# Feed-forward as 2x2 block products, seven in place of eight

## The reference

```python
D_FF = ((8 * D_MODEL // 3 + 255) // 256) * 256          # 2816

def swiglu_ffn(x, g, w_gu, w_down):
    h = rmsnorm(x, g) @ w_gu
    a, b = jnp.split(h, 2, axis=-1)
    return (jax.nn.silu(a) * b) @ w_down

# in each of the two layers, after the mixer:
x = x + swiglu_ffn(x, ffn_norm[layer], w_gate_up[layer], w_down[layer])
```

## Time and profile before

| | us |
|---|---|
| median of 3 runs (1864.62 to 1868.22) | 1866.26 |
| span of the profiled execution | 1864.6 |
| TensorE busy | 1815.1 |
| VectorE busy | 913.6 |
| ScalarE busy | 694.5 |
| GpSimd busy | 582.0 |

### The profile page before, as it was taken

The page is one execution under the profiler, slowest core; times in us unless marked ns, Lnnn a source line. Parts: engine busy times, 40 slices in busy tenths (PEclk is TensorE's granted clock), DMA queues, the critical chain, the costliest instruction groups (busy, mean ns, idle before and its releaser), DMA issues. The chain is left out here.

```text
span 1864.6 us, 41136 instructions
## 1 busy us (share of the span) xinstructions
PE 1815.1 (97%) x17185; PEld 1692.6 (91%) x17185; DVE 913.6 (49%) x1392; ACT 694.5 (37%) x1097; POOL 582.0 (31%) x298
## 2 busy tenths in 40 slices
PE   8999998999999999999998999999989999999998
PEld 7999997999999999999997677777779999999998
DVE  4757766345555521145653466655543555554000
ACT  5365455431221222245632555555544212222111
POOL 3333221243333343333531011221113333333332
PEclk9999999999999999999999999999999999999999
DMA  5333341222322232242356999999963222223222
GB/s 126 89 97 82 83 111 55 79 80 80 90 81 80 83 93 83 76 142 72 114 178 211 396 386 386 381 360 363 361 217 91 80 80 85 85 80 97 79 78 82
DMA packets 289101, 273.75 MB, mean 147 GB/s; under 512 B 19602, under 2 KB 250099, under 8 KB 288404
## 3 DMA queue, kind: packets, MB, share of 16 engines
q1 hardware_dynamic: 286980, 268.62, 44.1%
q10 hardware_dynamic: 1792, 1.44, 0.3%
q0 software_dynamic: 144, 1.05, 0.2%
HBM read 254.64 MB, written 16.43 MB: 145 GB/s over the span
## 5 line engine op out<-in xcount | busy, mean ns | idle before, releaser
L2020 POOL TENSOR_TENSOR a_wl<-a_wraw,a_wh 128x1024 fp32r<-128x1024 f32 (+2 forms) x91 | 233.5, 2566 | 401.1 <-ACT a_wh L1944 401.0
L2020 POOL TENSOR_TENSOR b_wl<-b_wraw,b_wh 128x1024 fp32r<-128x1024 f32 (+1 forms) x66 | 172.7, 2616 | 298.3 <-ACT b_wh L1944 298.3
L1901 PE MATMUL ps<-xh,a_wh 128*128 128x288 f32 x1104 | 238.4, 298 | 0.0
L1901 PE MATMUL ps<-xh,a_wl 128*128 128x288 f32 x1104 | 236.9, 296 | 0.0
L1901 PE MATMUL ps<-xl,a_wh 128*128 128x288 f32 x1104 | 236.8, 296 | 0.0
L1944 ACT ACTIVATE a_wh<-a_wraw 128x1024 fp32r<-128x1024 f32 (+2 forms) x91 | 100.6, 1106 | 335.5 <-PE ps L1901 315.4
L1944 ACT ACTIVATE b_wh<-b_wraw 128x1024 fp32r<-128x1024 f32 (+1 forms) x66 | 75.0, 1136 | 318.5 <-PE ps L1901 318.5
L2037 DVE TENSOR_TENSOR xT<-xT,ps 128x576 f32<-128x576 f32 x32 | 24.1, 754 | 320.8 <-PE ps L1901 320.8
L1901 PEld LDWEIGHTS ps<-xh,a_wh 128*128 128x128 f32 x1104 | 177.0, 187 | 1.1 <-issue 0.2
L1901 PEld LDWEIGHTS ps<-xh,a_wl 128*128 128x128 f32 x1104 | 177.2, 187 | 0.6
L1901 PEld LDWEIGHTS ps<-xl,a_wh 128*128 128x128 f32 x1104 | 177.2, 187 | 0.6
(11 more groups left out here) (352 smaller groups left out, 3880.6 us busy)
## 6 DMA issues: line engine op xcount, KB each, us to landing
a_wraw<-in_w_gate_up SPq DMA_DIRECT2D x44, 512.0 KB, 3.9
b_wraw<-in_w_gate_up SPq DMA_DIRECT2D x44, 512.0 KB, 3.8
xT<-in_cache_k SPq DMA_DIRECT2D x40, 512.0 KB, 6.4
xT<-in_cache_v SPq DMA_DIRECT2D x40, 512.0 KB, 6.9
a_wraw<-in_a_w_in SPq DMA_DIRECT2D x32, 512.0 KB, 4.2
f_h_plain<-in_cache_k SPq DMA_DIRECT2D x30, 512.0 KB, 6.1
xl_plain<-in_cache_v SPq DMA_DIRECT2D x30, 512.0 KB, 6.8
f_h_plain<-in_cache_v SPq DMA_DIRECT2D x30, 512.0 KB, 6.6
```

The source lines that it names most:

```text
L1901: mm = pe.matmul(ps[0:width(n), bank(n) + a, 0:HALF], wt[:, base(n) + t, 0:width(n)], ap[:, first + t, a * HALF:(a + 1) * HALF], start=kin ...
L2020: pool.tensor_tensor(part(wl, n), part(wraw, n), part(wh, n).bitcast(F32), ALU.subtract).then_inc(e["low"], 1)
```

## The change

The feed-forward's products become products of 2x2 blocks by Winograd's form of Strassen's method. A unit is now a pair: the gate and up tile of one hidden tile, or two neighbouring output tiles of the down product. Its weight is a 2x2 matrix of blocks (two column tiles; input tiles in pairs, even and odd), the activation is a 2x2 matrix too (input tiles even and odd; the two halves of the tokens), and the output's four blocks (two tiles, two halves) come from seven products instead of eight. Each product is still three matmuls of parts for each pair of input tiles: 12 matmuls for gate and up (four pairs), 9 or 6 for a down unit (three or two pairs).

Weights: seven blocks are loaded, of which four are targets of sums: S1 and S3 get A22 and a neighbour added by one transfer, S2 gets S1, S4 gets S2 (`add_operands`, transfers that GpSimd's queue issues and that add to what lies there). ScalarE rounds each operand three products ahead (`round_part`), into five slots; VectorE makes its low part two products ahead (`low_part`). GpSimd computes nothing in the feed-forward. Activations: each tile gives blocks and, for an odd one, combinations with the even one (`cross`, VectorE, one operation for an even and three for an odd tile), rounded by ScalarE (`round_combinations`) and made low by VectorE (`low_combinations`). Outputs: products share three banks a unit; of a gate-and-up unit ScalarE copies out three intermediate sums (`snapshot`) and VectorE makes the rest (`evict`), the gate in two banks of PSUM; of a down unit VectorE adds or subtracts all seven into `xT`.

The hidden width is cut in four chunks (4, 6, 6 and 6 tiles); the down product of a chunk (four units) stands behind the first gate-and-up unit of the next. The loads of unit m wait for the low parts of unit m - 2; the first unit's for the low part of output unit 7.

```diff
+A22, A11, S1, S3, A12, S2, S4 = range(7)
+
+
+def fast_products():
+
+    return ((A11, 0, 0), (S1, 1, 2), (S2, 4, 0), (A12, 2, 1), (S3, 5, 0), (S4, 3, 2), (A22, 6, 0))
...
+    chunks = [(0, 4), (4, 10), (10, 16), (16, KF)]
+    C = len(chunks)
+    ROWS = KD // 2
+    UNITS = [("o", f) for f in range(KD)]
+    for c, (first, end) in enumerate(chunks):
+        UNITS += [("g", i) for i in range(first + (1 if c else 0), end)]
+        if c < C - 1:
+            UNITS += [("g", end)]
+        UNITS += [("d", c, j) for j in range(ROWS)]
...
+    BANKS = ((0, 1, 2), (3, 6, 7))
+    SLOTS, AHEAD = 5, 3
...
+                def fetch(n):
+                    m, pairs = n - KD, pairs_of(n)
+                    if m == 0:
+                        sp.wait_ge(e["low"], KD)
+                    elif m == 1:
+                        sp.wait_ge(e["used"], KD)
+                    else:
+                        wait_low(sp, S * (m - 1))
...
+                    for dst, a, x in ((A11, 0, 0), (A22, 1, 1), (S1, 1, 0), (S3, 1, 0)):
+                        sp.dma_start(operand(m, dst), block(a, x)).then_inc(fetched[m % 2], 16)
+                    for dst, a, x in ((S2, 0, 0), (A12, 0, 1), (S4, 0, 1)):
+                        sp.dma_start(operand(m, dst), block(a, x)).then_inc(later[m % 2], 16)
...
+                    read = {2: 0, 4: 2, 5: 1, 6: 4}
+                    if pos in read:
+                        at = m, read[pos]
+                        if at in snap:
+                            pe.wait_ge(e["snapped"], snap[at] + 1)
+                        else:
+                            pe.wait_ge(e["taken"], take[at] + 1)
...
+                def product(n, pos):
+                    m, pairs = n - KD, pairs_of(n)
+                    which, b, _ = PRODUCTS[pos]
+                    s = S * m + pos
+                    banks_ready(n, pos)
+                    if pos in POOLED:
+                        pe.wait_ge(e["poollow"], m * len(POOLED) + POOLED.index(pos) + 1)
+                    else:
+                        wait_low(pe, s + 1)
+                    high, low = (slots[i][s % SLOTS] for i in range(2))
+                    for t, q in enumerate(pairs):
+                        tile = 2 * q if kind(n) == "g" else KD + 2 * q
+                        if m == 0 or kind(n) == "d" and UNITS[n][2] == 0:
+                            pe.wait_ge(e["comblow"], combined(tile) + (1 if b < 2 else 2 if b >= 4 else 3))
+                        at = slice(t * P, (t + 1) * P)
+                        for i, (wt, part) in enumerate(((high, 0), (high, 1), (low, 0))):
+                            mm = pe.matmul(place(m, pos), wt[:, at], combination(tile, part, b), start=pos in (0, 1, 3) and t == 0 and i == 0,
+                                           stop=t == len(pairs) - 1 and i == 2, skip_group_check=True)
+                    mm.then_inc(e["multiplied"], 1)
...
+                def round_part(s):
+                    if s >= S * F:
+                        return
+                    m, pos = divmod(s, S)
+                    which = PRODUCTS[pos][0]
+                    if s >= SLOTS:
+                        act.wait_ge(e["multiplied"], s - SLOTS + 1)
+                    if pos == 0:
+                        act.wait_ge(fetched[m % 2], m // 2 * 64 + 64)
+                    if which == A12:
+                        act.wait_ge(later[m % 2], m // 2 * 48 + 48)
+                    if which in sums:
+                        act.wait_ge(sums[which][m % 2], m // 2 * 16 + 16)
+                    act.activation(slot(s, 0), operand(m, which), ACT.Copy).then_inc(e["parthigh"], 1)
...
+                        if n == KD - 2:
+                            for s in range(AHEAD):
+                                round_part(s)
+                    elif n in fast:
+                        for pos in range(S):
+                            if kind(n) == "g" and pos < 3:
+                                snapshot(n, pos)
+                            round_part(S * (n - KD) + pos + AHEAD)
+                            if pos == (0 if own(n) else 2) and parted(n) is not None:
+                                round_combinations(KD + parted(n))
...
+                            if pos == 6:
+                                if kind(n) == "g":
+                                    silu(UNITS[n][1])
...
+                def add_operands(n):
+
+                    if n not in fast:
+                        return
+                    m = n - KD
+                    i, done = m % 2, m // 2 * 16 + 16
+                    pool.wait_ge(fetched[i], 4 * done)
+                    pool.dma_start(operand(m, S1, 2), operand(m, A22, 2), accum_op=ALU.add).then_inc(sums[S1][i], 16)
+                    pool.wait_ge(later[i], 3 * done)
+                    pool.wait_ge(sums[S1][i], done)
+                    pool.dma_start(operand(m, S2), operand(m, S1), accum_op=ALU.add).then_inc(sums[S2][i], 16)
+                    pool.wait_ge(sums[S2][i], done)
+                    pool.dma_start(operand(m, S4), operand(m, S2), accum_op=ALU.add).then_inc(sums[S4][i], 16)
...
+                def low_part(s):
+
+                    if s >= S * F or s % S in POOLED:
+                        return
+                    m, pos = divmod(s, S)
+                    dve.wait_ge(e["parthigh"], s + 1)
+                    dve.tensor_tensor(slot(s, 1), operand(m, PRODUCTS[pos][0]), slot(s, 0).bitcast(F32), ALU.subtract).then_inc(e["partlow"], 1)
...
+                def multiply(i, m):
+                    dst = odd if i % 2 else even
                     dve.wait_ge(e["scaled"], i + 1)
+                    dve.wait_ge(e["comblow"], combined(KD + i))
+                    dve.wait_ge(e["multiplied"], S * (m + 1))
+                    dve.tensor_tensor(dst[:, 0, :], kept[:, i % 2, 0, :], place(m, 6), ALU.mult).then_inc(e["taken"], 1)
+                    dve.tensor_tensor(dst[:, 1, :], kept[:, i % 2, 1, :], up[:, i % 2, :], ALU.mult).then_inc(e["product"], 1)
...
+                    if kind(n) == "o":
+                        if n == KD - 1:
+                            low_part(0)
+                            low_part(1)
                         add(n)
+                        cross(n)
+                        for g in range(len(groups(n))):
+                            low_combinations(n, g)
+                        if n > 0:
+                            accumulate(n)
+                    elif n in fast:
+                        i, t = mixed(n), parted(n)
+                        last = heads and n > TAIL - ROWS
+                        for pos in range(S):
+                            if pos == 0 and i is not None:
+                                multiply(i, n - 1 - KD)
+                                if own(n):
+                                    cross(KD + t)
+                            if kind(n) == "d" or pos in (3, 4, 5):
+                                evict(n, pos)
+                            if t is not None:
+                                if pos == 1 and not own(n):
+                                    cross(KD + t)
+                                if pos == (1 if own(n) else 4):
+                                    low_combinations(KD + t, 0)
+                                if pos == (1 if own(n) else 6) and t % 2:
+                                    low_combinations(KD + t, 1)
+                            if last and pos in (1, 2):
+                                low(2 * UNITS[n][2] - 3 + pos)
+                            if kind(n) == "g" and pos == 5:
+                                gated(n)
+                            low_part(S * (n - KD) + pos + 2)
...
+                            if kind(n) == "g" and pos == 6:
+                                scale_gate(UNITS[n][1])
```

More of the change, by code:

```diff
@@ new lines, in combination, with combinations, source, groups @@
+        def combination(t, part, b):
+            most, more, q = blocks_of(t, part)
+            return most[:, b, q, :] if b < 4 else more[:, b - 4, q, :]
+        def combinations(t, part, group):
+            most, more, q = blocks_of(t, part)
+            return (most[:, 0:2, q, :], more[:, 0:3, q, :], most[:, 2:4, q, :])[group]
+        def source(group):
+            return (even[:, 0:3:2, :], odd[:, 2:5, :], odd[:, 0:2, :])[group]
+        def groups(t):
+            return (1, 2) if t % 2 else (0,)
@@ L1824, in part, with operand @@
         def part(tile, n):
-            return tile[:, base(n):base(n) + depth(n), 0:width(n)]
+            first = plain(n) % 2 * KD
+            return tile[:, first:first + KD, 0:width(n)]
         def out(n):
             return ps[0:width(n), bank(n):bank(n) + 2, 0:HALF]
+        def operand(m, which, count=1):
+            w = len(pairs_of(KD + m)) * P
+            tile = (4 * which if which < A12 else {A12: 16, S2: 38, S4: 60}[which]) if m % 2 == 0 else 22 + 4 * which + (6 if which >= A12 else 0)
+            r, at = divmod(tile, KF)
```

(47 more changed lines are left out.)

379 lines of the change are left out of this document (253 added, 126 removed).

## The result

Median of before in the same series 1866.55 us, of the changed kernel 2149.26 us (2140.3 to 2153.8): ratio 1.150, 95% interval 1.147 to 1.154. Forecast was 1846.3 us, in a range of 1785 to 1930. It is slower by 283 us where 20 us of gain were forecast, and it lies beyond the upper end of the range by 219.

The account below looks back on a forecast made before the run. TensorE's instruction count was taken as the feed-forward's bound. Per layer, 52.8 us saved less 15.4, 5.5, 5.6, 2.0, 13.3 (entry) and 1.0 (end) left 10.0, 20.0 in both: 1846.3 us, range 1785 to 1930.

Parts of the forecast that it names:

- Matmuls removed: Feed-forward: 396 fewer matmuls a layer at an unchanged 0.1333 us each, 52.8 us a layer, 105.6 us gained in all.
- rival 4: Feed-forward products: fewer matmuls but each 1.5% longer, 11 us in all, 1857 us; put in the forecast's width.
- VectorE's order: Feed-forward: low parts queue behind evictions and other work, idling TensorE 15.4, 5.5, 5.6 and 2.0 us a layer.
- Rival 1: Feed-forward: VectorE's order costs nothing, only the entry and the end stay, 77 us gained, 1789 us; chance 0.20.
- The chain of sums: Feed-forward weights: S2 lands 12.0 us after its unit's loads are issued, S4 at 14.7; costed at nothing past the entry.
- The accumulation: Landing of one accumulating transfer: 4.0 us for 512 KB, 2.7 for 256 KB; upper bounds 6.9 and 5.2.
- The loads ahead of it: A unit's first four weight loads, 1.05 MB, were to take 5.3 us before the sums; all seven 7.8.
- The condition: Gate-and-up units: S2 must land within 13.0 us of its loads' issue; 12.0 forecast, so it fits by 1 us.
- The entry: Start of each layer's feed-forward: late loads and sums delay the first three products, 11.4 us plus 1.9 for clock, 13.3.
- The clock: At each layer's entry, TensorE's granted clock drops after idling; 1.9 us added there.
- Rival 2: Feed-forward: the accumulation chain sets the period, each accumulated byte costing the engines twice, 36 us a layer, 1918 us; chance 0.27.
- Rival 3: Sums' issue: busy VectorE delays GpSimd's descriptor writing 0.7 us a step, 2.1 us a chain, about 1865 us; chance 0.08.

Follow-up runs that it names:

- e6: Changed kernel without weight sums, each low part ahead of the eviction, and in output units ScalarE's weight rounding ahead of the residual tile: 1816.8 us, 0.974 of before.
- e5: Changed kernel without the weight sums, VectorE making the next low part ahead of the eviction: 1833.6 us, 0.982 of before.
- e1: Changed kernel with the weight sums left out, S1 to S4 staying as loaded: 1875.6 us, 1.006 of before.
- e2: Changed kernel with all three accumulating transfers adding A22, so none waits for another (wrong sums): 1997.2 us, 1.072 of before.
- e3: Changed kernel with its three transfers still in series but copying instead of adding (sums left out): 2015.3 us, 1.080 of before.
- e12: Changed kernel, complete, low parts ahead of evictions, weight rounding ahead of combinations, only S2 computed by GpSimd: 1924.9 us, 1.033 of before.
- e8: Kernel before plus a tail of lone SBUF-to-SBUF accumulating and copying transfers, run once for its rows: 512 KB accumulations 4.8 us, copies 3.15.
- e11: Changed kernel, complete, low parts ahead of evictions, weight rounding ahead of combinations, S2 and S4 computed by GpSimd: 1911.4 us, 1.024 of before.
- e4: Changed kernel, complete, GpSimd computing all the weight sums instead of accumulating transfers, order unchanged: 1995.5 us, 1.069 of before.
- e10: Changed kernel, complete, GpSimd computing all weight sums, low parts ahead of evictions, weight rounding ahead of combinations: 1994.2 us, 1.068 of before.

## Why the prediction was wrong, point by point

- **Matmuls removed, 105.6 us:** the count is right, 16393 for 17185. At its 0.1333 us they would leave 1815.1 - 105.6 = 1709.5 us of busy TensorE; e6, where it seldom waits, has 1723.9 with a granted clock of 0.988. The term holds within 15 us, so rival 4 (matmuls 1.5% longer, 11 us) can be no more than about its own size.
- **VectorE's order, (15.4 + 5.5 + 5.6 + 2.0) x 2 = 57 us:** mechanism right, size near. e5 gives 42 us back; product 6 was stalled 0.69 us, 0.7 forecast; two-pair down units took 7.3 us in e1 (7.0 forecast), three-pair ones 9.06 (8.86). The gate-and-up unit is 12.2 to 12.3, not 11.9, and still 11.6, not 11.2, without the stall. Rival 1 is out: the order costs.
- **The chain of sums, costed at nothing past the entry:** this is the step that failed. It cost 274 us, its share of the entries included. In six units S2 was there 18.5 to 21.0 us after the loads were issued, not 12.0, against the 13.0 allowed. Two of its terms were too low. The accumulation: near the lower bound I took 4.0 and 2.7 us, because rows lie in SBUF and are long; alone it is 4.8 and 3.6, and in the kernel medians are 5.5 to 5.8 and 3.3 to 4.9, inside the bounds (up to 6.9 and 5.2), and over the 5 us that were named as the sign of a wrong price. The loads ahead of it: 7.4 and 8.5 us for 5.3 in the two units shown, where I let the first four move alone, and the engines are 0.79 busy. GpSimd's issue, 0.86 us for each step, is contained in the accumulations' times. The condition was well put (13.0 us from issue to S2), but it had 1 us to spare while my own upper bounds lay 2.9 + 2.5 us above the values taken up to S2. A condition with less margin than its inputs have width can't be costed at nothing.
- **The entry, 13.3 us a layer:** too low at each step. First product at 391.4 (385.6 forecast), second at 399.1 (390.4), third at 410.6 (397.7). It began late: TensorE's stalls in the output units weren't foreseen. ScalarE's rounding stands behind the tile's combinations, and GpSimd's low part behind it:

```profile
352.39 0.78 PE L2042 MATMUL ps<-f_h,a_wh 128*128 128x288 f32 x4 [1.77 <-POOL a_wl L2296]
368.69 0.76 PE L2042 MATMUL ps<-f_h,a_wh 128*128 128x288 f32 x4 [1.76 <-POOL a_wl L2296]
383.36 2.02 SPq L1982 DMA_DIRECT2D a_wraw<-in_w_gate_up  x4
390.26 1.02 POOL L2272 DMA_DIRECT2D a_wraw<-a_wraw  x1 [6.92 <-DMA a_wraw<-in_w_gate_up]
397.53 0.87 POOL L2275 DMA_DIRECT2D a_wh_plain<-a_wraw  x1 [6.25 <-DMA a_wraw<-a_wraw]
404.01 0.86 POOL L2277 DMA_DIRECT2D a_wl_plain<-a_wh_plain  x1 [5.61 <-DMA a_wh_plain<-a_wraw]
410.60 3.22 PE L2080 MATMUL ps<-f_l 128*128 128x288 f32 x12 [8.22 <-ACT t_small L2200]
```

  The loads are issued at 383.36 (378.8 forecast), then S1 takes 7.3 us and S2 6.5 from start to start. Undoing the order in the output units gave 17 us (e6 against e5), about 8 a layer. I had costed that order only once, at the last unit.
- **The clock:** I costed it at the entry alone, 1.9 us. With 43 waits of over 2 us of TensorE in the 76 units (one in e1), it is paid everywhere: the mean granted clock is 0.937 in the changed kernel and 0.987 in e1, and the same 16393 matmuls are busy 1837.7 us against 1763.9. So 74 of the 274 us are not the waiting itself but slower matmuls after it.
- **Rival 2, 0.27, 1918 us:** the right mechanism, at less than a fifth of its size: 283 us slower where it had 51. Its byte price was right (twice; measured 2.15), yet it took the engines' time as the bound, 12.9 us a unit. The engines were 0.79 busy, short of full, and a unit 15.4: what set it was the length of the series (15.2 by the estimate above). Most of its links are longer than alone; that the traffic beside them does it is the likely reading, not tried apart. e2 and e3 give 152 and 134 us for one cause each, e12 puts most of it at S2.
- **Rival 3** (GpSimd's descriptors held back, 0.7 us a step): not tried by itself. In gate-and-up units nearly every issue takes 0.85 to 0.91 us, as in e8 with VectorE at rest (0.85 to 0.98), so most were not held back. S1's issue in the down units takes 1.20 us, and single ones up to 1.58, some of them close behind another issue; for what reason stays open.
- **What no run settles:** how much of the lengthening of an accumulation in the kernel (5.8 for 4.8 us, up to 4.9 for 3.6) is the loads, and how much other accumulations; and why e1, without any sum, stays 29 us above my forecast. The output units are 17 us of it, the gate-and-up units, 0.3 to 0.4 us longer, 44 times 0.35 = 15, the down units, 24 times 0.2 and 8 times 0.3, 7. That is 39, more than 29; part comes back at the entry, where e1 has no sums to wait for (first product at 392.3, 6.7 us later than forecast, third at 400.4, only 2.7). All this is arithmetic on the rows, not an experiment.

## What to carry to other kernels

Where work moves from an engine to a series of transfers, write out its length from issue to use with the widest price of each link; if the margin is smaller than that width, price the miss, including the slower matmuls behind each wait. Before adding to every weight tile in flight, ask which link is wanted first, and compute that one on an idle engine: here that one sum, taken first, carried 162 of 176 us. And each instruction moved ahead in an in-order queue must be costed at every unit where it stands in front, not at the last one alone.

## What the runs showed of the hardware

- An accumulating transfer within SBUF runs at 208 GB/s behind 2.3 us fixed, a copy at about 420 behind 1.9; its issue holds GpSimd 0.86 us, a copy's 0.54 (e8). In use, 168 against 360 GB/s of the engines' time (the changed kernel, e3).
- GpSimd's sums of 128x512, 1.3 to 1.9 us each, are quicker than the transfer that they replace (3.3 to 4.9 us in the kernel, 3.6 alone), yet they lengthen VectorE's low parts of the same size from 0.69 us to means of 0.74 to 0.90 (e11), 0.91 to 1.03 (e4) and 0.82 to 1.27 (e10), and leave its operations with an input in PSUM at 0.45 us (e10).
- Repeated waits of 2 to 8 us take the granted clock down over a whole kernel, from 0.987 (e1, where but one of the waits in the feed-forward is over 2 us) to 0.937, worth 74 us at the same count of matmuls.
